# A feed loop for the expert products with its loads issued in another order

## What the reference computes

```python
def one_block(args):
    xb, ib, gb = args
    u = expert_u[ib]
    a = jax.nn.gelu(jnp.einsum('thkd,td->thk', u, xb).astype(jnp.float32), approximate=False)
    w = (gb * a).astype(expert_v.dtype)
    return jnp.einsum('thk,thkd->td', w, expert_v[ib])
```

## Time and profile before

| | us |
|---|---|
| median of 3 runs | 3408.54 |
| lowest and highest | 3404.97 and 3410.98 |
| the profiled execution's own time | 3404.97 |
| span of that execution (first to last instruction) | 3403.2 |
| stage `experts` in the span | about 929 to 1993 |

### The profile page before, as it was taken

How to read it: one execution, slowest core, us unless ns; L and a number is a source line. 1 busy time by engine, 2 the same in 40 slices (tenths; PEclk the granted TensorE clock), 3 DMA queues, 4 the chain that set the end, 5 groups by cost and what they waited for, 6 DMA issues and landing times. The chain is left out here.

```text
span 3403.2 us, 33869 instructions
## 1 busy us (share of the span) xinstructions
PE 2861.6 (84%) x12218; PEld 2114.6 (62%) x12218; DVE 1665.4 (49%) x3057; ACT 950.2 (28%) x1583; POOL 786.8 (23%) x661
## 2 busy tenths in 40 slices
PE   4976878626599999999999968965895799999995
PEld 2444667425489999999999956743674344444442
DVE  4334547899876667777777755255231000000002
ACT  2013432125533333333333332253331011111101
POOL 0000032355443333333333314301211000000001
PEclk7977989869899999999999979977896899999997
DMA  7610022203498888888888832110200899999995
GB/s 230 223 53 16 1 72 79 85 8 142 170 319 279 281 278 276 274 276 278 279 280 279 277 113 75 50 52 3 92 33 28 318 343 336 334 333 333 333 326 187
DMA packets 282119, 658.88 MB, mean 194 GB/s; under 512 B 36380, under 2 KB 87324, under 8 KB 280732
## 3 DMA queue, kind: packets, MB, share of 16 engines
q1 hardware_dynamic: 234412, 485.60, 40.7%
q0 software_dynamic: 42992, 155.23, 13.6%
q10 hardware_dynamic: 4608, 16.78, 1.2%
HBM read 609.23 MB, written 48.30 MB: 193 GB/s over the span
## 5 line engine op out<-in xcount | busy, mean ns | idle before, releaser
L2373 PE MATMUL bank<-w,moe_xt 128*128 128x512 f32 x1024 | 452.0, 594 | 2.2 <-DMA w<-in_w 2.2
L1485 PE MATMUL bank<-h_hi,u_hi 128*128 128x384 f32 x1024 | 344.2, 336 | 7.3 <-DVE u_lo L1557 7.3
L2424 DVE TENSOR_TENSOR moe_xt<-bank,moe_gain 128x512 f32<-128x512 f32 x64 | 41.3, 686 | 623.6 <-PE bank L2363 623.6
L1485 PE MATMUL bank<-h_hi,u_lo 128*128 128x384 f32 x1024 | 344.0, 336 | 0.0
L1485 PE MATMUL bank<-h_lo,u_hi 128*128 128x384 f32 x1024 | 343.6, 336 | 0.0
L2373 PEld LDWEIGHTS bank<-w,moe_xt 128*128 128x128 f32 x1024 | 192.8, 191 | 233.1 <-issue 230.3
L209 POOL TENSOR_TENSOR w_lo<-ring,w_hi 128x512 fp32r<-128x512 f32 (+1 forms) x136 | 173.3, 1306 | 565.5 <-ACT w_hi L199 565.5
L1497 PE MATMUL bank<-v_hi,peer_w_lo 128*128 128x512 f32 x768 | 300.0, 391 | 0.0
L1497 PE MATMUL bank<-v_lo,peer_w_hi 128*128 128x512 f32 x768 | 299.9, 390 | 0.0
L1497 PE MATMUL bank<-v_hi,peer_w_hi 128*128 128x512 f32 x768 | 298.7, 389 | 0.0
L1472 POOL DMA_INDIRECT got_rows<-in_u_rows,diff x128 | 190.3, 1487 | 326.2 <-DVE got_rows L1564 296.8
(11 more groups left out here) (470 smaller groups left out, 4925.6 us busy)
## 6 DMA issues: line engine op xcount, KB each, us to landing
w<-in_w SPq DMA_DIRECT2D x64, 2048.0 KB, 19.4
u_in<-in_u_tiles SPq DMA_DIRECT2D x128, 512.0 KB, 4.8
v_in<-in_expert_v SPq DMA_DIRECT2D x128, 512.0 KB, 7.0
w_slot<-in_w SPq DMA_DIRECT2D x32, 2048.0 KB, 10.0
ada_in<-in_w_ada SPq DMA_DIRECT2D x48, 512.0 KB, 4.9
gates_by_key<-spread SPq DMA_DIRECT2D x6, 4096.0 KB, 12.1
gate_in<-gates_by_key SPq DMA_DIRECT2D x384, 64.0 KB, 4.9
ring<-in_w_in SPq DMA_DIRECT2D x11, 2048.0 KB, 8.2
```

The lines of the kernel that those rows point to most:

```text
L1485: last = pe.matmul(g.bank[e][:, 0:DENSE_T], u[:, e, c], h[:, k, :], start=(n == 0), stop=(n == 3 * DC - 1))
L2373: last = pe.matmul(g.bank[2 if which == 1 else 3][:, :], self.xt[:, par, k, :], self.w13[par][0 if which == 1 else 1][:, k, :], start=(k = ...
```

## The change

SyncE's list for the stage is written as one loop. In round q it now issues u(q,0), v(q,0), u(q,1), v(q,1) and then the six gate loads. The same loads with the same waits are issued, the same number of times; only their order on the queue is another. No other engine's list changes.

```diff
-                def up_in(q):
+                for q in range(Q):
                     for e in range(GT):
+                        n = (q - 1) * GT + e + 1
+                        t = q * GT + e
                         if q >= 1:
-                            sp.wait_ge(s["j_ulo"], (q - 1) * GT + e + 1)
-                        sp.dma_start(u_in[:, e, :], a["u_tiles"][q * GT + e].rearrange("p c e -> p (c e)")).then_inc(s[f"j_u{e}"], 16)
-
-                def down_in(q):
-                    for e in range(GT):
+                            sp.wait_ge(s["j_ulo"], n)
+                        sp.dma_start(u_in[:, e, :], a["u_tiles"][t].rearrange("p c e -> p (c e)")).then_inc(s[f"j_u{e}"], 16)
                         if q >= 1:
-                            sp.wait_ge(s["j_vlo"], (q - 1) * GT + e + 1)
-                        t = q * GT + e
+                            sp.wait_ge(s["j_vlo"], n)
                         sp.dma_start(v_in[:, e, :], a["expert_v"][0, t * P:(t + 1) * P, :]).then_inc(s[f"j_v{e}"], 16)
-
-                def gates_in(q):
                     if q >= 2:
                         sp.wait_ge(s["j_w"], (q - 1) * GT)
                     for b in range(DENSE_T // GB):
                         sp.dma_start(gate_in[:, q % 2, b], gates[b, :, q * GT:(q + 1) * GT, :]).then_inc(s[f"j_g{q % 2}"], 16)
-                up_in(0)
-                for q in range(Q):
-                    down_in(q)
-                    gates_in(q)
-                    if q < Q - 1:
-                        up_in(q + 1)
```

## The result

The changed kernel takes 3430.77 us (median of 4 runs, 3419.09 to 3435.85) against 3409.39 us before (4 runs): 1.006 times as long, 95% interval 1.0032 to 1.0088. It was forecast slower, at 3448.5 us: the sign and the mechanism hold, the size is about half of what I gave (21 us for 40). The interval spans 11 to 30 us.

A forecast was written before the change was run, and what follows sets the result against it. TensorE was taken to bound the kernel at 16.55 us a round; rounds of 16.8 and 17.6 us made it 49.4 us late, less 9.5 of cushion: 40 us, so 3448.5 us, 80% range 3404 to 3490.

The forecast's parts named there:

- What bounds the kernel, and what moves: `experts` stage: TensorE sets the 16.55 us round; only u(q,1) loses, its lead falling from 14.2 to 5.9 us.
- The circle: From v(q,0)'s issue through u(q,1)'s landing, ScalarE and VectorE to v(q+1,0)'s issue: 16.8 us first half, 17.6 second.
- The landing time L: u(q,1)'s time from issue to landing behind v(q,0): 7.8 us taken for all rounds, bounded by 6.7 and 8.6.
- The cushion: TensorE takes the last `u_lo` tile 9.5 us after it is done; taken off the 49.4 us of lateness.
- Hidden anyway: Rival: u(q,1) lands in 7.2 us or less, so time is 3405 to 3415 us, no change; chance 0.22.
- More contention: Rival: u(q,1) lands in 8.6 us, rounds take 17.6 and 18.4 us, 89 us slower in all, 3497; chance 0.12.
- The clock: Rival: TensorE's idle gaps drop its clock to 1.2 GHz, costing some hundreds of microseconds; chance 0.01.
- Faster: Rival: at the start, another landing order saves at most the 7.3 us TensorE waits for `u_lo`; chance 0.03.
- Signs that I had wrong: Expected in the profile: TensorE waits for `u_lo` about 60 times, some 45 us; ScalarE's `u_hi` waits for every second tile.

The follow-up runs named there:

- the longer circle: One more VectorE operation of 128x1024, result unused, after the gathered rows of each round, added to the changed kernel: 3514.73 us, ratio 1.0316.

## Why the prediction was right, and where not

**What bounds the kernel, and what moves**: held for the first 41 rounds. There only u(q,1) came late; u(q,0) and the v loads went out where they were said to. The 8 us to spare that I gave u(q,0) were gone from round 41 on: ScalarE, no longer held by TensorE ahead of `v_hi`, reaches that tile 12.1 us after v(q,0)'s issue, where it was 18.7 before, and waits:

```profile
1843.68 1.06 ACT L1515 ACTIVATE u_hi<-u_in 128x1024 fp32r<-128x1024 f32 x1 [0.45 <-DMA u_in<-in_u_tiles]
```

It isn't on the circle, since VectorE takes this `u_hi` only behind the `v_lo` pair, at 1850.30. The first round in which u(q,1)'s place counts is where I put it too: v(2,0) went out at 959.87 (forecast 961.2).

**The circle**: held, in its legs, its length and its place, as the table and the two kernels that cut it (deeper `v_in`; rows moved) show.

**The landing time L is the term that was mis-sized.** I took 7.8 us for all rounds. What I had wrong is the first of its two parts. u(q,1) lands behind v(q,0) in all 64 rounds, on average 1.9 us later in both halves. But I counted v(q,0)'s own landing as before. Taken one by one, it had means of 6.5 us in the first half and 6.7 in the second; in the changed kernel it has 5.5 and 6.0. The rows of L1449, for v loads issued from 960 to 1470, then from 1490 to 1970 (the trace has the landings of v(q,0) alone):

```profile
DMA to landing us min/median/max: 4.0/5.2/7.3
...
DMA to landing us min/median/max: 5.5/6.1/6.7
```

With 6.5 and 6.7 L would have been 8.0 and 8.2, near my 7.8. L itself was 7.07 on average in the first half. The circle was then 0.4 + 7.07 + 8.6 = 16.1 us there, under TensorE's 16.55, and bound only in single rounds (L reaches 9.4). v(33,0) went out at 1467.43 against 1466.10 before: a round of 16.37 us over 31 rounds, not 16.8. In the second half L was 7.6 and the round 17.30, not 17.6. Over 31 and 30 rounds these two differences, with the 1.3 us at v(2,0), are the 23.6 us by which v(63,0), issued at 1986.43, was ahead of my 2010.0. Why v(q,0) lands sooner than before, and soonest in the first half, stays open. The v loads' medians of before, 7.1 and 7.0, gave no hint of it. The gathers matter for it, as shown, but a little less in the first half (0.3 us for half of their bytes, against 0.7), and GpSimd takes longer to issue them in the first half (1617 ns against 1499 in the changed kernel); that these are linked was not tried.

**The cushion**: here the reasoning failed in one step. I wrote that the circle forbids its being built up. It did so only as far as the circle bound in the first half, which it hardly did: TensorE never waited from 960 to 1500. So most of the cushion was there at the midpoint: the second half's 30 rounds cost 23 us and TensorE gave out only 16. The step isn't in the sum, which takes the 9.5 us off at the end, but the signs rest on it (below). `u_lo` of u(63,1) ended 25.8 us late (1996.9 against 1971.14), less the 9.5 of cushion: 16.3 us. TensorE's last matmul of the stage starts at 2017.4 against 2000.9, 16.5 us. (So before, the stage ran to about 2001 and not to 1993.) With v(33,0) at 1467.4 and L = 7.6 put in, the prediction's sum gives 1467.4 + 30 x 17.4 + 10.3 - 1971.1 - 9.5 = 19 us instead of 40 (10.3 is 0.4 + 7.6 + 2.3, from v(63,0)'s issue to the end of `u_lo`); the rest is the 0.1 us by which a circle's sum is longer than the measured round.

The other 7 us of the two spans' difference of 23.4 fall after the stage, in code that is the same. From that matmul to the end of the span it is 1402.3 us before and 1409.2 in the changed kernel. The ten experiments, whose code there is the same, have 1399.0 to 1409.4, so this is within the scatter of single executions. Of the 21 us between the medians the trace thus shows 16.5 in the stage; that the rest is scatter is likely but not shown.

**The other rivals.** *Hidden anyway* describes the first half: with L near 7.1 the cost was within 0.2%. *More contention* didn't come by itself, but the longer circle and the u behind both v loads show it at once when the phase shifts. *The clock*: the granted clock stayed at 1.00 in each window of 100 us from 1000 to 1900. With larger gaps it gave a little; windows of the kernel with u behind both v, columns as in the earlier trace rows:

```profile
1200.00:1300.00 100.00, 90.28 (x431) 81.48 (x430) 55.45 (x80) 27.98 (x40) 34.72 (x20) 0.95 0.71 242
```

TensorE busy for 90 us of 100, granted 0.95: nothing like the halving that I priced, in a kernel with longer gaps than I had priced it for. *Faster* had no case. The Trainium skill's formula for one DMA ("DMA: Bandwidth & Descriptors", section "Anatomy of one DMA") is fitted to single transfers issued through GpSimd. Carried over to these loads, which SyncE issues, it gave 4.0 us by estimate for u(q,1), with the two loads alone. Measured among the gathers it was 7.1 to 7.6, and the change was not hidden.

**Signs that I had wrong**: the trace puts down 18 waits of TensorE for `u_lo` (17.2 us), not 60 and 45 us, since they begin only once the cushion is used up, eight rounds into the second half, at 1617 (16 of them after 1500). And ScalarE waits for every second tile only up to round 40; from 41 on it waits for both.

## What to carry to other kernels

A queue that issues loads for several buffers should follow the order in which the buffers come free. One load put behind a later wait can close a circle of wait, landing and compute that has nothing to do with the engine that sets the pace; its cost is (its length less the pace) per round, less what cushion the engine that sets the pace has, and nothing where it is shorter than the pace. To find its length, follow the load's issue to its user and on to whatever lets the queue go on, and take the landing time from loads that go out at that moment, among the same traffic; where there are none, as here, give the landing of the load in front a range of its own, since the change can move that too. Three cures did equally well here: the order of before, a deeper buffer for the wait in front, or moving work out of the circle to the time in which the load is under way.

## What the runs showed that I had not expected

Landing times of the same 512 KB depend on the moment of issue as much as on the place in the queue: 7.1 to 7.6 us in the changed kernel, 8.2 with half the rows to work off, 8.25 with 1.15 us of work added (first half), 9.15 one place further back, and 6.8 to 6.9 among gathers of half the size. An engine with room to spare is no safe place for work either: 1.15 us a round cost nothing in the kernel before and 84 us in the changed one.
